# Between two transformer blocks: the last merge in PSUM, Fourier heads on unnormed tokens, both norms as one factor

## The chip, the cores and the metric

The kernel runs on one core of a Trainium2 chip. The time is the device time of one execution in microseconds (us), read as the median of several executions. TensorE (PE) multiplies matrices into PSUM, whose eight banks hold 512 f32 values per partition. VectorE (DVE) and ScalarE (ACT) read and write both PSUM and SBUF, GpSimd (POOL) works in SBUF only, and SyncE (SP) issues the transfers.

## The reference, cut to what matters

Two layers of a network, one after the other, on 256 tokens of width 1024. Around the change it computes:

```python
merged = jnp.sum(g * branch_d, axis=2)          # four branches, each times its gate
x1 = x + merged @ w_out                         # end of the first block
x2 = rms_norm(x1, final_g)                      # x1 * rsqrt(mean(x1^2) + 1e-6) * final_g
h = jnp.concatenate([meta, x2], axis=1)         # 16 meta tokens in front: 272
hn = rms_norm_2(h, norm1_g)                     # the second norm, of the normed tokens
f_in, qkv, z, ab, gate_f, gate_d = jnp.split(hn @ w_in, points, axis=-1)
fg = f_in.reshape(bsz, seq_len, 4, 128)         # four Fourier heads, then fft2 of each
```

The second block goes on with a gated delta rule over `qkv` and `ab`, and ends in a mixture of 64 experts whose weights are read from HBM.

## The kernel before, in words

Tokens stand transposed: channels in the 128 partitions, `KD` = 8 chunks of channels, tokens (`SEQ` = 256, with the meta tokens `LEN` = 272) in the free dimension. `res` holds `h`, with the 16 meta tokens in its first columns (`META`). Each engine's order is the order in which its function is written, with semaphores between them.

Every f32 product of a weight and the activations is made of three passes over rounded parts, high times low, high times high, low times high (`matmul3`, L415 to L417). So each operand is first split in a high part (a rounded copy) and a low part (the rest). Weights come in quarters of 512 KB: ACT makes the high part (L1202), POOL the low part (L2385), two quarters to a half, three halves in flight. ACT converts a half (`lead`, `lead_for`) at fixed places of its program, once the last reader of the half three before it is done. Projections go through PSUM banks 0 to 2 in turn (`PJ`), small things through banks 3 to 7 (`WK`).

The stretch of the change:

1. The last of the four branches, `br1`, is projected into four banks (two chunks each). For each, DVE multiplies by the gate (L1849), adds to `merged` (L1850), and splits the sum (L1644, L1645). The output projection `wo0` to `wo3` (48 passes each) needs all eight chunks before it can finish its first bank.
2. For each `wo` bank DVE adds the bank to `res` (L1859) and ACT squares the sum (L1325). Then PE sums the squares over the channels with a matrix of ones (`ssq2`, L455), DVE and ACT make the factor of the first norm as a full 128x256 tile (L1637, L1328, L1639), DVE applies it (L1864), ACT squares again (L1333), PE sums again (`ssq3`), DVE and ACT make the factor of the second norm (L1869, L1336, L1871), and for each chunk DVE writes the high part, the unrounded value and the low part of `hn` (L1874 to L1876).
3. PE projects the Fourier heads `fin0` to `fin3` (24 passes each, 272 columns), which wait chunk by chunk for L1876; ACT takes them out (L1339). Then comes `ab` (72 passes, three runs over 16, 128 and 128 tokens, 32 columns each) with its weight `w_ab` split by DVE (L1878), then the keys.
4. DVE takes `ab` out (L1886), ACT makes the softplus of it (L1347 to L1350), and DVE's convolutions of the keys follow (L1904, L1908).

The transfers of the second block's constants (`dft_d`, `dft_l`, `w_ab`, `tri`, `level`) wait in SP's order for the first norm (`final`, L2449).

## Time and profile before

| | |
|---|---|
| median of 3 runs | 1308.05 us (1307.49 to 1309.38) |
| the profiled execution | 1311.39 us, its span 1309.5 us |
| PE busy | 1129.7 us, 86% of the span |
| DVE, ACT, POOL busy | 489.4, 376.5, 385.2 us |
| chain that ended last | PE 60%, DMA 19%, DVE 13%, ACT 2% |
| mean granted TensorE clock | 0.925 of full speed |

The span is the profile's own time; the execution's time is 1.89 us longer. A busy share of an engine is a mean over stretches with different limits. The granted clock is told in tenths of 2.4 GHz in the page, and as a share in the view by windows (1.00 or 0.50, or a mix where it changed within the window).

### The profile page before, as it was taken

What the parts mean: (1) busy time and instruction counts of PE and PEld (TensorE: products, weight loads), DVE (VectorE), ACT (ScalarE), POOL (GpSimd) and SP (SyncE); (2) the same over time, 40 slices, a digit from 0 to 9 for tenths busy, and PEclk for the clock granted to TensorE, in tenths of its full rate; (3) what the DMA queues carried; (4) which work ended last, traced back from release to release, by engine and by line L of the source; (5) the groups of instructions that cost most, each with busy time, mean ns of one, the idle gap of its engine ahead of it and who ended that gap; (6) DMA issues with size and microseconds to landing.
All of it is one profiled execution on the core that took longest, in us unless ns stands there. A gap on an engine that the chain in (4) does not pass through costs nothing.

```text
span 1309.5 us, 20191 instructions
## 1 busy us (share of the span) xinstructions
PE 1129.7 (86%) x8332; PEld 906.7 (69%) x8332; DVE 489.4 (37%) x924; ACT 376.5 (29%) x540; POOL 385.2 (29%) x175
## 2 busy tenths in 40 slices
PE   9998999999978799988999999787767677776776
PEld 7977999999977797988888978643433333343343
DVE  3415743702262456543886332322221111221122
ACT  5524253434424175433434210301101010100101
POOL 5725668888855235433103000000000000000000
PEclk9988899999978799998999999699998888999887
DMA  7623536566644224222312137979999999999993
GB/s 260 182 65 102 156 120 198 152 180 188 181 142 129 89 82 129 73 90 65 129 65 73 59 106 312 423 280 428 428 429 428 428 427 427 428 427 429 427 429 129
DMA packets 39533, 304.30 MB, mean 232 GB/s; under 512 B 4645, under 2 KB 5029, under 8 KB 26026
## 3 DMA queue, kind: packets, MB, share of 16 engines
q1 hardware_dynamic: 39178, 302.82, 61.0%
q8 instruction: 49, 0.80, 0.3%
q10 hardware_dynamic: 288, 0.52, 0.1%
q14 instruction: 18, 0.15, 0.0%
HBM read 302.28 MB, written 1.05 MB: 232 GB/s over the span
## 4 chain that ended last, share of the span: by engine, by line
PE 60%; DMA 19%; DVE 13%; issue 2%; ACT 2%; SPq 1%; POOL 1%; DVEq 0%; ACTq 0%
PE bank L415 10%; PE bank L416 10%; PE bank L417 10%; DMA arena<-gate_up 9%; DMA weights<-gate_up 6%; PE bank L730 6%; PE bank L1150 6%; DMA arena<-down 4%; PE bank L1163 3%; DVE arena L1908 2%; PE bank L1135 1%; PE bank L1172 1%; DVE arena L2070 1%; DVE arena L2068 1%; POOL rounded L2385 1%
## 5 line engine op out<-in xcount | busy, mean ns | idle before, releaser
L2385 POOL TENSOR_TENSOR rounded<-weights,rounded 128x1024 fp32r<-128x1024 f32 x152 | 370.8, 2465 | 259.3 <-ACT rounded L1202 250.2
L415 PE MATMUL bank<-rounded 128*128 128x256 f32 (+2 forms) x784 | 227.2, 290 | 16.6 <-POOL rounded L2385 7.2
L417 PE MATMUL bank<-rounded 128*128 128x256 f32 (+2 forms) x784 | 225.5, 288 | 0.0
L416 PE MATMUL bank<-rounded 128*128 128x256 f32 (+2 forms) x784 | 225.4, 288 | 0.0
L1202 ACT ACTIVATE rounded<-weights 128x1024 fp32r<-128x1024 f32 x146 | 146.6, 1050 | 114.8 <-PE bank L417 92.6
L415 PEld LDWEIGHTS bank<-rounded 128*128 128x128 f32 (+1 forms) x784 | 151.7, 194 | 20.9 <-POOL rounded L2385 8.1
L415 PE MATMUL bank<-rounded,rounded 128*128 128x256 f32 (+3 forms) x472 | 141.3, 301 | 12.3 <-DVE rounded L1876 6.6
L416 PEld LDWEIGHTS bank<-rounded 128*128 128x128 f32 (+1 forms) x784 | 151.2, 193 | 0.3 <-issue 0.2
L417 PEld LDWEIGHTS bank<-rounded 128*128 128x128 f32 (+1 forms) x784 | 150.9, 192 | 0.3
L416 PE MATMUL bank<-rounded,rounded 128*128 128x256 f32 (+3 forms) x472 | 138.1, 294 | 0.0
L417 PE MATMUL bank<-rounded,rounded 128*128 128x256 f32 (+3 forms) x472 | 138.0, 294 | 0.0
L730 PE MATMUL bank<-arena,weights 128*128 128x256 f32 x512 | 116.0, 385 | 0.1
L730 PEld LDWEIGHTS bank<-arena,weights 128*128 128x128 f32 x512 | 97.1, 193 | 15.3 <-issue 1.5
L415 PEld LDWEIGHTS bank<-rounded,rounded 128*128 128x128 f32 (+1 forms) x472 | 94.3, 200 | 16.7 <-issue 6.5
L1135 PE MATMUL bank<-arena 128*128 128x128 f32 x512 | 73.1, 311 | 36.6 <-DVE arena L2343 36.6
L1135 PEld LDWEIGHTS bank<-arena 128*128 128x128 f32 x512 | 70.2, 224 | 42.7 <-issue 42.7
L416 PEld LDWEIGHTS bank<-rounded,rounded 128*128 128x128 f32 (+1 forms) x472 | 94.1, 200 | 0.1
L417 PEld LDWEIGHTS bank<-rounded,rounded 128*128 128x128 f32 (+1 forms) x472 | 94.0, 199 | 0.0
L1150 PE MATMUL bank<-arena 128*32 128x512 f32 x512 | 64.6, 663 | 22.1 <-DMA arena<-gate_up 20.7
L1150 PE MATMUL bank<-weights,arena 128*32 128x512 f32 x512 | 63.9, 655 | 21.8 <-DMA weights<-gate_up 19.9
L1163 PE MATMUL bank<-arena 128*32 128x512 f32 x512 | 61.4, 622 | 11.8 <-ACT arena L1597 6.6
L1172 PE MATMUL bank<-arena 128*128 128x256 f32 x256 | 59.5, 386 | 13.0 <-DVE arena L2355 13.0
(409 smaller groups left out, 1272.8 us busy)
## 6 DMA issues: line engine op xcount, KB each, us to landing
weights<-front SPq DMA_DIRECT2D x152, 512.0 KB, 4.1
weights<-gate_up SPq DMA_DIRECT2D x32, 2048.0 KB, 31.8
arena<-down SPq DMA_DIRECT2D x32, 2048.0 KB, 19.7
arena<-gate_up SPq DMA_DIRECT2D x32, 2048.0 KB, 32.1
weights<-front SPq DMA_DIRECT2D x8, 2048.0 KB, 7.8
arena<-hcatT SPq DMA_DIRECT2D x1, 1088.0 KB, 5.1
arena<-dft_l SPq DMA_DIRECT2D x1, 768.0 KB, 4.2
arena<-ln_rows SPq DMA_DIRECT2D x1, 512.0 KB
```

The source lines that it names most:

```text
L415: nc.tensor.matmul(out, a[0], b[1], start=start, stop=False)
L416: nc.tensor.matmul(out, a[0], b[0], start=False, stop=False)
L417: return nc.tensor.matmul(out, a[1], b[0], start=False, stop=stop)
L730: last = nc.tensor.matmul(f.bank[:, j * n:(j + 1) * n], w[:, c:c + P], x[:, k, :], start=k == 0, stop=k == KD - 1)
L1135: last = nc.tensor.matmul(o, m_tok[:, t, k * P:(k + 1) * P], pick_m[:, t, :], start=t == 0, stop=t == TT - 1)
L1150: last = nc.tensor.matmul(banks[3][j * CAP:(j + 1) * CAP, :], xg[:, k, j * CAP:(j + 1) * CAP], gate_up[u][j][:, k * 2 * FE:(k + 1) * 2 * F ...
L1163: last = nc.tensor.matmul(banks[5 + half][j * CAP:(j + 1) * CAP, :], hid_T[:, i, j * CAP:(j + 1) * CAP], down[j // 2][:, c:c + 512], start ...
L1172: last = nc.tensor.matmul(banks[b][:, j * SEQ:(j + 1) * SEQ], yb[:, c:c + P], pick_T, start=True, stop=True)
L1202: nc.scalar.activation(w_hi[h % SPLIT][:, quarter(q)], raw[q % RAW], ACT.Copy).then_inc(sem("w_hi"), 1)
L1908: link(nc.vector.scalar_tensor_tensor(dst[:, lo:hi], x[:, first + lo + s:first + hi + s], tap(j), dst[:, lo:hi], ALU.mult, ALU.add))
L2068: link(nc.vector.tensor_tensor(o, pairs[:, k, k + 1:32].unsqueeze(2).to_broadcast([P, below, upto]), inv[:, k, 0:upto].unsqueeze(1).to_bro ...
L2385: nc.gpsimd.tensor_tensor(lo, raw[q % RAW], hi.bitcast(f32), ALU.subtract).then_inc(sem("w_lo"), 1)
```

## The change

- **The merges.** DVE's product with the gate is written back into the PSUM bank it came from. For the last branch the sum is also left in the bank; ACT copies it out as the rounded high part, DVE subtracts for the low part.
- **The tokens between the blocks.** For each `wo` bank DVE adds `res` in place in the bank (`x1`). ACT writes it to `res`, and its rounded product with both gains (`both_g` = `final_g` times `norm1_g`) to `raw_hi_r`; DVE writes the low part `raw_lo_r`. ACT squares `x1` with and without `final_g` into banks 5 and 6, and DVE adds the pairs up in `sum_g` and `sum_x`.
- **The Fourier heads** multiply these unnormed tokens. Both norms together are one factor per token, 1/sqrt(sum_g/D + eps*(sum_x/D) + eps^2) (`factors2`), which DVE puts on each head's result as it takes it out (`take_fourier`).
- **The sums** are 128x2 columns now (`sums`), one square root and one reciprocal of 128x4; `token_rows` spreads them over the partitions (`rows12`, `rows1`). PE's order is `fin0`, `sums`, `fin1`, `rows12`, `rows1`, `fin2`, `fin3`, `ab`.
- **`hn`** is made through banks 5 and 6, high part by ACT, low part by DVE. The first norm on `res` comes last before `ab`.
- **The meta tokens** are normed at the kernel's start (`meta_n`): a square on ACT, 8 small matmuls in place of one of the products that PE runs there on zeros (`warm_up`), and 11 small DVE instructions.
- SP's transfers of the constants wait for the last `raw_lo_r` (`normed`, 16) instead of `final`.

The diff without the renumbered semaphore values; "..." also marks removed lines, which stand in the functions above:

```diff
+        SQ_BANKS, HN_BANKS = (5, 6), (5, 6)
...
+        RAW_AT = layer_base + 2 * KD * LEN
+        raw_hi_r, raw_lo_r = (rounded(RING + RAW_AT + i * KD * LEN, KD * LEN).rearrange("p (k t) -> p k t", k=KD) for i in range(2))
+        sum_x, sum_g = (arena[:, RAW_AT + 2 * KD * LEN + i * 512:RAW_AT + 2 * KD * LEN + (i + 1) * 512] for i in range(2))
+        both_g, factors2 = stat(KD), stat(2 * TT)
+        meta_n = tri[:, 0:KD * META].rearrange("p (k t) -> p k t", k=KD)
+        meta_sq = arena[:, gates_at + 1024:gates_at + 1024 + KD * META].rearrange("p (k t) -> p k t", k=KD)
...
-            warm_up(banks[5], 1)
+            f = begin("rms_rows", (2,))
+            pe.wait_ge(sem("squares"), 5)
+            for k in range(KD):
+                nc.tensor.matmul(f.bank[:, SEQ:SEQ + META], ones, meta_sq[:, k, :], start=k == 0, stop=k == KD - 1)
             pe.wait_ge(sem("rstd"), 1)
-            token_rows("rms_rows", rstd1, (2,))
+            token_rows(f, rstd1)
             warm_up(banks[5], 2)
...
+                          ready=lambda k: ("merged", 4 * 3 + 2 * (k // 2) + 2))
             hn_all = hn_hi_r, hn_lo_r
             hn_x = [m[:, :, META:] for m in hn_all]
...
+
+            def fourier_in(g):
+
+                project_T([f"fin{g}"], FIN, (raw_hi_r, raw_lo_r), LEN, per=1, column=g * P,
+                          ready=(lambda k: ("normed", KD + k + 1)) if g == 0 else None)
+
+            fourier_in(0)
+            f = begin("sums")
+            for s, src in enumerate((sum_g, sum_x)):
+                pe.wait_ge(sem("sq_pairs"), 12 + s)
+                for t in range(TT):
+                    for i in range(2):
+                        last = nc.tensor.matmul(f.bank[:, 2 * s + t:2 * s + t + 1], src[:, i * SEQ + t * P:i * SEQ + (t + 1) * P],
+                                                ones[:, 0:1], start=i == 0, stop=i == 1)
+            end(f, last)
+            fourier_in(1)
+            pe.wait_ge(sem("rstd"), 2)
+            token_rows(begin("rows12"), factors2[:, 0:TT])
+            token_rows(begin("rows1", (7,)), factors2[:, TT:])
+            fourier_in(2)
+            fourier_in(3)
             pe.wait_ge(sem("second_in"), 16 * 5)
...
+            pe.wait_ge(sem("normed"), 3 * KD + 1)
             f = begin("ab")
...
+            nc.scalar.activation(meta_sq, res[:, :, 0:META], ACT.Square).then_inc(sem("squares"), 1)
             for q in (0, 1): quarter_hi(q)
...
             norm_hi(3)
-            for q in (4, 5): quarter_hi(q)
+            quarter_hi(4)
+            act.wait_ge(sem("variance"), 2)
+            nc.scalar.activation(meta_var, meta_var, ACT.Sqrt).then_inc(sem("deviation"), 1)
...
+                lead_for(f"br{ORDER[3]}{j}")
+                act.wait_ge(sem("merged"), 4 * 3 + 2 * j + 1)
+                nc.scalar.activation(h1_hi_r[:, 2 * j:2 * j + 2, :], two(fills[f"br{ORDER[3]}{j}"].bank),
+                                     ACT.Copy).then_inc(sem("h_hi"), 1)
+            for j in range(4):
                 lead_for(f"wo{j}")
                 act.wait_ge(sem("x1"), j + 1)
...
+                x1 = two(fills[f"wo{j}"].bank)
+                if j == 0:
+                    link(nc.scalar.activation(raw_hi_r[:, :, 0:META], meta_n, ACT.Copy))
+                pair = res[:, 2 * j:2 * j + 2, META:]
+                link(nc.scalar.activation(pair, x1, ACT.Copy))
+                for i, k in enumerate((2 * j, 2 * j + 1)):
+                    last = nc.scalar.activation(raw_hi_r[:, k, META:], x1[:, i, :], ACT.Copy, scale=both_g[:, k:k + 1])
+                last.then_inc(sem("h_hi"), 1)
+                if j > 0:
+                    act.wait_ge(sem("sq_pairs"), 5 + 2 * j)
+                of_g, of_x = (two(banks[b]) for b in SQ_BANKS)
+                for i, k in enumerate((2 * j, 2 * j + 1)):
+                    last = nc.scalar.activation(of_g[:, i, :], pair[:, i, :], ACT.Square, scale=col("final_g", k))
+                last.then_inc(sem("squares"), 1)
+                nc.scalar.activation(of_x, pair, ACT.Square).then_inc(sem("squares"), 1)
+            lead_for("fin0")
+            nc.scalar.activation(spare[:, 0:1], ones[:, 0:1], ACT.Sqrt)
+            lead_for("sums")
+            f = fills["sums"]
+            act.wait_ge(sem("variance"), 5)
+            nc.scalar.activation(f.bank[:, 8:8 + 2 * TT], factors2, ACT.Sqrt).then_inc(sem("deviation"), 1)
+            for part_hi, part_raw in ((hn_hi_r, raw_hi_r), (hn_lo_r, raw_lo_r)):
+                nc.scalar.activation(part_hi[:, :, 0:META], part_raw[:, :, 0:META].bitcast(f32), ACT.Copy)
+            lead_for("fin2")
             for j in range(4):
...
+                act.wait_ge(sem("h_rows"), 4 + j + 1)
+                nc.scalar.activation(hn_hi_r[:, 2 * j:2 * j + 2, META:], two(banks[HN_BANKS[j % 2]]), ACT.Copy).then_inc(sem("h_hi"), 1)
+            lead_for("fin3")
...
                     norm_rows(j + 2)
             dve.wait_ge(sem("normed"), KD)
+            dve.sem_inc(free[sums.b], 1)
+            nc.vector.tensor_scalar(meta_var, row_bank.bank[:, SEQ:SEQ + META], 1.0 / D, EPS, ALU.mult,
+                                    ALU.add).then_inc(sem("variance"), 1)
+            link(nc.vector.tensor_tensor(both_g, cols[:, COLS["final_g"][0]:COLS["final_g"][1]],
+                                         cols[:, COLS["norm1_g"][0]:COLS["norm1_g"][1]], ALU.mult))
+            dve.wait_ge(sem("deviation"), 2)
+            meta_row = row_bank.bank[:, SEQ + META:SEQ + 2 * META]
+            link(nc.vector.reciprocal(meta_row, meta_var))
+            for k in range(KD):
+                last = nc.vector.scalar_tensor_tensor(meta_n[:, k, :], res[:, k, 0:META], col("norm1_g", k), meta_row,
+                                                      ALU.mult, ALU.mult)
+            link(last)
             dve.sem_inc(free[row_bank.b], 1)
...
+                        dve.sem_inc(free[f.b], 1)
+                        dve.sem_inc(sem("merged"), 1)
+                        continue
+                    link(nc.vector.tensor_tensor(two(f.bank), two(f.bank), g, ALU.mult))
+                    if i < 3:
+                        link(nc.vector.tensor_tensor(m, two(f.bank), m, ALU.add))
+                        dve.sem_inc(free[f.b], 1)
+                        dve.sem_inc(sem("merged"), 1)
+                        continue
+                    link(nc.vector.tensor_tensor(two(f.bank), two(f.bank), m, ALU.add))
+                    dve.sem_inc(sem("merged"), 1)
+                    dve.wait_ge(sem("h_hi"), 4 + j + 1)
+                    js = slice(2 * j, 2 * j + 2)
+                    link(nc.vector.tensor_tensor(merged_lo_r[:, js], two(f.bank), h1_hi_r[:, js].bitcast(f32), ALU.subtract))
                     dve.sem_inc(free[f.b], 1)
...
                     dve.sem_inc(sem("merged"), 1)
             for j in range(4):
                 f = got(f"wo{j}")
...
+                x1 = two(f.bank)
+                link(nc.vector.tensor_tensor(x1, x1, res[:, 2 * j:2 * j + 2, META:], ALU.add))
+                dve.sem_inc(sem("x1"), 1)
+                dve.wait_ge(sem("h_hi"), 8 + j + 1)
+                if j == 0:
+                    link(nc.vector.tensor_tensor(raw_lo_r[:, :, 0:META], meta_n, raw_hi_r[:, :, 0:META].bitcast(f32), ALU.subtract))
+                for i, k in enumerate((2 * j, 2 * j + 1)):
+                    last = nc.vector.scalar_tensor_tensor(raw_lo_r[:, k, META:], x1[:, i, :], both_g[:, k:k + 1],
+                                                          raw_hi_r[:, k, META:].bitcast(f32), ALU.mult, ALU.subtract)
+                link(last)
+                dve.sem_inc(sem("normed"), 2)
                 dve.sem_inc(free[f.b], 1)
...
+                for s, dst in enumerate((sum_g, sum_x)):
+                    dve.wait_ge(sem("squares"), 5 + 2 * j + s + 1)
+                    b = banks[SQ_BANKS[s]]
+                    if j == 0:
+                        link(nc.vector.tensor_copy(dst, b[:, :]))
+                    else:
+                        link(nc.vector.tensor_tensor(dst, b[:, :], dst, ALU.add))
+                    dve.sem_inc(sem("sq_pairs"), 1)
+
+            sums = got("sums")
+            of_g, of_x = sums.bank[:, 0:TT], sums.bank[:, TT:2 * TT]
+            nc.vector.tensor_scalar(factors2[:, TT:], of_x, 1.0 / D, EPS, ALU.mult, ALU.add)
+            link(nc.vector.tensor_scalar(factors2[:, 0:TT], of_x, EPS / D, EPS * EPS, ALU.mult, ALU.add))
+            nc.vector.scalar_tensor_tensor(factors2[:, 0:TT], of_g, 1.0 / D, factors2[:, 0:TT], ALU.mult,
+                                           ALU.add).then_inc(sem("variance"), 1)
+            dve.wait_ge(sem("deviation"), 5)
+            link(nc.vector.reciprocal(factors2, sums.bank[:, 8:8 + 2 * TT]))
+            dve.sem_inc(sem("rstd"), 1)
+            dve.sem_inc(free[sums.b], 1)
+            rows12 = got("rows12")
+
+            def hn_rows(j):
+
+                for i, k in enumerate((2 * j, 2 * j + 1)):
+                    last = nc.vector.scalar_tensor_tensor(banks[HN_BANKS[j % 2]][:, i * SEQ:(i + 1) * SEQ], res[:, k, META:],
+                                                          both_g[:, k:k + 1], rows12.bank[:, 0:SEQ], ALU.mult, ALU.mult)
+                last.then_inc(sem("h_rows"), 1)
+
+            def hn_low(j):
+
+                dve.wait_ge(sem("h_hi"), 12 + j + 1)
+                pair = slice(2 * j, 2 * j + 2)
+                link(nc.vector.tensor_tensor(hn_lo_r[:, pair, META:], two(banks[HN_BANKS[j % 2]]),
+                                             hn_hi_r[:, pair, META:].bitcast(f32), ALU.subtract))
+                dve.sem_inc(sem("normed"), 2)
+
+            def take_fourier(g):
+
+                f = got(f"fin{g}")
+                nc.vector.tensor_tensor(f_T[:, g, META:], f.bank[:, META:LEN], rms2[:, 0:SEQ], ALU.mult)
+                link(nc.vector.tensor_copy(f_T[:, g, 0:META], f.bank[:, 0:META]))
+                dve.sem_inc(free[f.b], 1)
+                dve.sem_inc(sem("f_T"), 1)
+
+            hn_rows(0)
+            hn_rows(1)
+            link(nc.vector.tensor_copy(rms2[:, 0:SEQ], rows12.bank[:, 0:SEQ]))
+            take_fourier(0)
+            hn_low(0)
+            hn_rows(2)
+            take_fourier(1)
+            hn_low(1)
+            hn_rows(3)
+            hn_low(2)
+            hn_low(3)
+            take_fourier(2)
+            take_fourier(3)
+            dve.sem_inc(free[rows12.b], 1)
+            f = got("rows1")
             for k in range(KD):
...
+                last = nc.vector.scalar_tensor_tensor(res[:, k, META:], res[:, k, META:], col("final_g", k), f.bank[:, 0:SEQ],
+                                                      ALU.mult, ALU.mult)
+            link(last)
             dve.sem_inc(free[f.b], 1)
...
+            dve.wait_ge(sem("h_hi"), 17)
+            link(nc.vector.tensor_tensor(w_ab_lo_r, w_ab, w_ab_hi_r.bitcast(f32), ALU.subtract))
             dve.sem_inc(sem("normed"), 1)
...
                 if h == 2 * FIN + 3:
-                    sp.wait_ge(sem("final"), KD)
```

How the instructions move. In DVE's order, the last of the four last merges, what follows it, and the first norm, before (bank0 to bank2 are PSUM banks, arena is SBUF, rounded a rounded part in SBUF):

```order
L1849 TENSOR_TENSOR arena<-bank1,arena 128x512
L1850 TENSOR_TENSOR arena<-arena 128x512
L1644 CAST rounded_20120_2048<-arena 128x512
L1645 TENSOR_TENSOR rounded_49952_2048<-arena,rounded_20120_2048 128x512
L1859 TENSOR_TENSOR arena<-arena,bank2 128x2x256
L1859 TENSOR_TENSOR arena<-arena,bank0 128x2x256
L1859 TENSOR_TENSOR arena<-arena,bank1 128x2x256
L1859 TENSOR_TENSOR arena<-arena,bank2 128x2x256
L1637 TENSOR_SCALAR arena<-bank7 128x256
```

And the same place in the changed kernel, from the last of the merges to the second `wo` bank:

```order
L1909 TENSOR_TENSOR bank1<-bank1,arena 128x512
L1915 TENSOR_TENSOR bank1<-bank1,arena 128x512
L1919 TENSOR_TENSOR rounded_49952_2048<-bank1,rounded_20120_2048 128x512
L1925 TENSOR_TENSOR bank2<-bank2,arena 128x512
L1929 TENSOR_TENSOR rounded_26648_2176<-arena,rounded_24472_2176 128x8x16
L1931 SCALAR_TENSOR_TENSOR rounded_26648_2176<-bank2,arena,rounded_24472_2176 128x256 x2
L1940 COPY arena<-bank5 128x512
L1940 COPY arena<-bank6 128x512
L1925 TENSOR_TENSOR bank0<-bank0,arena 128x512
```

The merge has three DVE instructions instead of four, none with two inputs in SBUF, and between two `wo` banks DVE now has five more.

On ACT, around the last `wo` bank, before:

```order
L1202 ACTIVATE rounded_4096_2048<-weights 128x1024 x2
L1325 ACTIVATE arena<-arena 128x512
L1202 ACTIVATE rounded_6144_2048<-weights 128x1024 x2
L1328 ACT_TABLE_LOAD
L1328 ACTIVATE arena<-arena 128x256
L1333 ACTIVATE arena<-arena 128x544 x4
L1336 ACTIVATE arena<-arena 128x272
```

and now:

```order
L1227 ACTIVATE rounded_4096_2048<-weights 128x1024 x2
L1363 ACTIVATE arena<-bank2 128x2x256
L1365 ACTIVATE rounded_24472_2176<-bank2,arena 128x256 x2
L1371 ACTIVATE bank5<-arena 128x256 x2
L1373 ACTIVATE bank6<-arena 128x512
L1227 ACTIVATE rounded_6144_2048<-weights 128x1024 x2
L1375 ACT_TABLE_LOAD
L1375 ACTIVATE arena<-arena 128x1
L1379 ACTIVATE bank7<-arena 128x4
```

The one square of a bank has become six instructions, all ahead of the next half of the weights, and the table of the square root is loaded by an instruction that waits for no sum.

The last DVE instructions ahead of `ab` are these in the changed kernel (before, they were the three lines L1874 to L1876 eight times, and the split of `w_ab`):

```order
L1968 TENSOR_TENSOR rounded_34840_2176<-bank5,rounded_20120_2176 128x2x256
L1968 TENSOR_TENSOR rounded_34840_2176<-bank6,rounded_20120_2176 128x2x256
L1975 TENSOR_TENSOR arena<-bank2,arena 128x256
L1976 COPY arena<-bank2 128x16
L1975 TENSOR_TENSOR arena<-bank0,arena 128x256
L1976 COPY arena<-bank0 128x16
L1996 SCALAR_TENSOR_TENSOR arena<-arena,bank7 128x256 x8
L2001 TENSOR_TENSOR rounded_37480_256<-arena,rounded_37736_256 128x256
L2009 TENSOR_TENSOR arena<-bank4,arena 16x16
```

The take-out of the heads and the first norm of `res` now stand on DVE between the last low part of `hn` and `w_ab`, for which `ab` waits.

## Rows read from the trace of the kernel before

**Rows 1.** Windows: start:end, us, PE, PEld, DVE, ACT, POOL busy (instructions), clock, DMA, GB/s
```profile
240.00:320.00 80.00, 80.00 (x669) 80.00 (x669) 24.81 (x22) 34.12 (x38) 67.22 (x28) 1.00 0.60 180
...
375.00:387.00 12.00, 4.25 (x18) 3.48 (x18) 10.91 (x11) 1.54 (x2) 5.62 (x3) 0.68 0.51 156
387.00:393.00 6.00, 5.66 (x26) 5.67 (x27) 0.23 (x1) 0.00 (x0) 0.00 (x0) 0.50 0.00 0
393.00:411.00 18.00, 18.00 (x152) 17.97 (x151) 2.21 (x4) 7.59 (x9) 12.80 (x6) 1.00 0.39 117
...
430.00:440.00 10.00, 7.79 (x25) 5.68 (x26) 9.44 (x23) 0.00 (x0) 0.00 (x0) 0.53 0.01 2
440.00:445.00 5.00, 5.00 (x26) 5.00 (x26) 0.00 (x0) 0.40 (x1) 0.00 (x0) 0.58 0.00 0
```

**Rows 2.** Timeline of DVE and POOL, last merges: start, us, engine, line, [idle before, releaser]
```profile
365.90 0.69 DVE L1849 TENSOR_TENSOR arena<-bank,arena 128x512 f32<-128x512 f32 x1 [24.09 <-PE bank L417]
...
374.24 1.83 DVE L1850 TENSOR_TENSOR arena<-arena 128x512 f32<-128x512 f32 x1
376.22 2.35 DVE L1644 CAST rounded<-arena 128x512 fp32r<-128x512 f32 x1 [0.15 <-DVE arena L1850]
378.61 2.71 DVE L1645 TENSOR_TENSOR rounded<-arena,rounded 128x512 fp32r<-128x512 f32 x1
...
386.54 0.69 DVE L1645 TENSOR_TENSOR rounded<-arena,rounded 128x512 fp32r<-128x512 f32 x1
...
375.67 5.10 POOL L2385 TENSOR_TENSOR rounded<-weights,rounded 128x1024 fp32r<-128x1024 f32 x2 [0.15 <-ACT rounded L1202]
```

**Rows 3.** Timeline, PE's first `wo` matmuls and DVE's first take-out of `wo`
```profile
376.23 0.36 PE L415 MATMUL bank<-rounded 128*128 128x256 f32 x1 [1.73 <-POOL rounded L2385]
...
381.43 0.58 PE L415 MATMUL bank<-rounded 128*128 128x256 f32 x1 [4.25 <-DVEq L1855]
...
387.34 0.58 PE L415 MATMUL bank<-rounded 128*128 128x256 f32 x1 [1.30 <-DVEq L1855]
...
393.73 0.69 DVE L1859 TENSOR_TENSOR arena<-arena,bank 128x512 f32<-128x512 f32 x1 [6.50 <-PE bank L417]
```

**Rows 4.** Timeline from the last `wo` matmul to the first of `fin0`
```profile
410.66 3.61 PE L455 MATMUL bank<-arena 128*128 128x256 f32 x16
...
412.27 1.99 ACT L1202 ACTIVATE rounded<-weights 128x1024 fp32r<-128x1024 f32 x2
...
414.28 1.28 ACT L1328 ACT_TABLE_LOAD   x1
...
416.02 1.75 DVE L1639 RECIPROCAL arena<-arena 128x256 f32<-128x256 f32 x1 [1.29 <-ACT arena L1328]
...
430.09 0.36 PE L415 MATMUL bank<-rounded,rounded 128*128 128x272 f32 x1 [4.51 <-DVE rounded L1876]
```

**Rows 5.** Windows, columns as in rows 1: `fin2` and `fin3`; `ab` at either clock
```profile
445.00:450.70 5.70, 5.70 (x48) 5.70 (x47) 0.00 (x0) 2.80 (x4) 3.83 (x2) 1.00 0.09 9
...
451.50:454.40 2.90, 2.90 (x33) 2.90 (x30) 0.00 (x0) 2.00 (x2) 1.63 (x2) 1.00 0.79 232
454.60:459.10 4.50, 4.50 (x23) 4.50 (x23) 0.00 (x0) 0.00 (x0) 2.93 (x2) 0.50 0.58 152
```

**Rows 6.** Timeline, DVE's take-out of `ab`
```profile
459.28 0.16 DVE L1886 TENSOR_TENSOR arena<-bank,arena 16x16 f32<-16x16 f32 x1 [19.56 <-PE bank L417]
```

**Rows 7.** Timeline of the kernel's start: the norm of the first block
```profile
7.93 1.95 PE L470 MATMUL bank<-arena 128*128 128x1 f32 x16
...
10.83 0.71 PE L478 MATMUL bank<-arena 128*128 128x128 f32 x4
...
11.70 1.67 DVE L1666 SCALAR_TENSOR_TENSOR bank<-arena,bank 128x256 f32<-128x256 f32 x4 [0.92 <-PE bank L478]
...
12.61 0.60 ACT L1237 ACTIVATE rounded<-bank 128x512 fp32r<-128x512 f32 x1 [2.03 <-DVE bank L1666]
```

**Rows 8.** Waits of SP's queue: who waited for whom, us in total, times, longest
```profile
SPq L2439 <- POOL rounded L2385: 538.9, 146, 33.2
```

71 lines of the change are left out of this document (16 added, 55 removed).

## The prediction

> **What bounds the kernel now.** I read the busy shares by slices first, then the waits, then the timeline from 365 to 475 us, then windows with the granted clock. From 240 to 320 us PE is busy for 80.00 of 80 us at the full clock [rows 1]: there only PE's own work counts, and the merges of the first three branches lie under it. From 375 to 387 us PE is busy 4.25 us of 12 [rows 1]. The reader is to see why: after its last `br1` matmul PE waits for the merges, and two DVE instructions of 128x512 last 2.35 and 2.71 us while POOL runs; the same split lasts 0.69 us once POOL is done [rows 2]. The output projection runs from 387.34 us on [rows 3]. Then comes a serial chain from its end (410.66 us) to the first Fourier matmul (430.09) [rows 4], then heads paced by DVE at half clock: 25 matmuls' worth of PE time in 10 us [rows 1]. SP's queue for the front weights waits for POOL, not for the memory (538.9 us in 146 waits) [rows 8], and the expert stage starts on signals of this same chain. So a microsecond cut here should be one at the end.
>
> I measure in three pieces: up to T0, the end of `wo0` (393.6 us, where DVE takes it) [rows 3]; from T0 to the first matmul of `ab` (450.8) [rows 5], 57.2 us; and `ab` itself, to 459.1 [rows 6].
>
> **Piece 1, the last merges.** Before, four DVE instructions each. Now DVE multiplies (0.69), adds (0.69), ACT copies 128x512 out of PSUM (0.60) [rows 7], DVE subtracts (0.69); with some 0.15 us for each of four hand-offs, 3.3 us a bank. From 365.9 [rows 2] the four end at 369.2, 372.5, 375.8 and 379.1. The half of the weights that ACT converts in between (2.0 us [rows 4]) fits between the second and the third copy. PE can run chunks 0 to 5 of `wo0` as they come and the last two from 379.3 instead of 387.34: 8.0 us. (The row at 376.23 names POOL as releaser of `wo0`; the bank of the second merge came free at that very moment, so I take it to be that [rows 3].)
>
> The clock: before, PE idled 1.73, then 4.25 us around six matmuls [rows 3], the clock fell to 1.2 GHz, and 26 of the 30 matmuls left to `wo0` ran at 5.66/26 = 0.22 us instead of 18.00/152 = 0.12 [rows 1]. Now one idle stretch of 2.5 us remains; I take the clock to hold. The 30 matmuls then take 3.6 instead of 6.2 us: 2.6 more. T0 is 382.9: **10.6 us** in all. That the new operation, a DVE instruction that reads and writes one bank, costs 0.69 is a choice: the nearest rows read a bank (0.69) and write another (1.67 for four halves, 0.42 each) [rows 2, 7]; the lower bound is 0.69, the upper the slowest DVE row of that size, 2.71.
>
> **Piece 2, from T0 to `ab`.** `wo0` to `wo3` stay 3 x 5.7 = 17.1 us apart (48 x 0.118) [rows 1]. ACT's work per bank grows from one square to a copy, two scaled copies and three squares, 2.8 us, and two weight quarters, 2.0: 4.8 of 5.7 us. It hides; but the half for `wo3` now starts 3 us later and is split (two POOL quarters, 5.1 us [rows 2], or less) about 1 us before PE asks. If that cover is gone, each us of delay is one on the path.
> After T0+17.1: DVE's add with its hand-off until 18.0; ACT, then done with a half, copies `x1`, then twice scaled, to 19.6; DVE's two low parts to 20.6; PE, which has done chunks 0 to 5, finishes `fin0` at 21.5. ACT's squares end at 21.0, DVE's two sums of pairs at 22.3. The eight sum matmuls are recorded as 16, 1.95 us [rows 7]; the second four start at 22.5 and end at 23.5. PE goes on with `fin1` (24 x 0.12 = 3.0 [rows 5]) to 26.5. Beside it DVE prepares the factors (24.3), ACT has loaded the root's table (1.28 [rows 4]) by then, and the factors stand at 25.1: hidden by 1.4 us. `rows12` is 0.71 [rows 7]: DVE starts at 27.3.
> Now DVE is late, and what is queued on it ahead of `ab` sets the end: products for `hn` 8 x 0.42 = 3.3 [rows 7], a copy 0.45, four low parts at 0.69 + 0.15 = 3.4, four take-outs of a head at some 0.78 (a product of 256, a copy of 16, two signals) = 3.1, 0.2 for ACT's last copy, eight products for `res` at 0.41 = 3.3, `w_ab`'s low part 0.45, hand-offs 0.35: 14.6 us, to T0+41.9. PE ends `fin3` at 33.8 and idles 8 us. 57.2 - 41.9 = **15.3 us**. What goes: the 128x256 reciprocal (1.75) and its double, two sums of 16 recorded matmuls (3.61 and more), the table load on the path (1.28) [rows 4], and the pacing of `fin0`.
>
> `w_ab`'s low part is the last instruction here with two inputs in SBUF. POOL works on the next half from about T0+36.6 to 41.3, and rows 2 show such an instruction at 2.71 instead of 0.69 beside POOL, while L1849 with an input in PSUM stayed at 0.69. I count nothing and keep 2.0 us as upper bound. The Trainium skill (SBUF — State Buffer, SBUF: two separate sides) says that a DVE instruction with two SBUF inputs and a GpSimd instruction exclude each other for a whole instruction. By that rule the sum would be up to 2 us worse where the two meet, and the saving of the merges is right as I have it.
>
> **Piece 3, `ab` itself.** Before, it began at the full clock and fell in the middle: 0.11 us per matmul of 32 columns, then 0.21 (both windows count the edges) [rows 5]. After 8 us of idle PE it now starts at 1.2 GHz, as it did after 387 us [rows 1]. Of its 48 wide-weight matmuls 26 change rate: 26 x 0.10, and 24 small ones some 0.6 in all: **3.2 us lost**. Lower bound 0, if the clock holds.
>
> **The start.** The square of the meta tokens (128x128, some 0.3 us) stands ahead of ACT's weight quarters, which had 0.2 us of slack: 0.1 lost. The root and the 10 small DVE instructions come where both wait for PE. SP's constants move ahead by as much as the chain; nobody waits for them. Merges of branches 2 and 3: nothing, PE is full.
>
> **Sum** against the profiled execution (1311.4): 10.6 + 15.3 - 3.2 - 0.1 = 22.6, so 1288.8 for a profiled execution of that kind; the runs shown have their median 3.3 below it, so 1308.05 - 22.6 = **1285.4 us**.
>
> **Rivals.**
> 1. *The short gaps drop the clock too.* PE would be near idle in `wo0` for 2.5 us and around `fin0` and the sums for 4 us with six wide matmuls between, and six matmuls did not hold it before [rows 3]. For it: that row. Against: each gap is shorter. Price: 2.6 in `wo0` and 2.0 in `fin1` (24 x 0.08); and at the start, where one of the zero products goes, up to 2. With the first two, 1290.0.
> 2. *`ab` keeps the full clock*, or PE is released earlier: 1282.2. The idle 8 us speak against it.
> 3. *Absorbed later.* A stage behind is bound by something that doesn't move with this chain. Rows 8 speak against it. If half were lost, 1296.7.
> 4. *Slower: in-place PSUM instructions are dear.* The place: the last merges (two in series per bank), DVE's x1 after the last bank, and, above 2.0 us each, the earlier merges, whose banks come every 2.9 us. At D us each the path gains 9 x (D - 0.69) + 8 x (D - 2.0); from D = 2.7 on, the gain of 22.6 is gone. At 3.5 us it would be 25.3 + 12.0 = 37.3 lost, 1322.8. Rows 2 show reads of a bank at 0.69, rows 7 writes at 0.42 per half: nothing hints at four times that.
>
> **How the numbers follow.** The forecast 0.66 (its own range 1282 to 1289), rival 1 0.20, rival 2 0.06, rival 3 0.05, rival 4 0.03. About 0.2% (2.6 us) is what a measurement of this kernel can tell from no change. Faster: all but rival 4 and a tail of rival 3, 0.95; same 0.02; slower 0.03. The range takes in rivals 1 and 2, w_ab's 2 us and hand-offs I priced by eye: 1280.5 to 1292.5.
>
> **What would show it.** In the profile of the changed kernel: the DVE instructions of the last merges at 0.69; the first matmul that follows the last merge at 379.3 us and the clock at 1.00 behind it; `wo0` ends near 383; `fin0` with one wait of about 1 to 2 us; `rows12` directly behind `fin1`; PE idle for about 8 us before `ab`, released by DVE's L2001; `ab` at about 424.8 us and 11.5 us long; and the same distances as before from `ab` to the end. The forecast is wrong if wide-matmul stretches behind `wo0` or in `fin1` show 1.2 GHz, if PE waits for weights at `wo3`, or if the distance from `ab` to the end grows.

## The result: 1292.4 us, 16.4 us faster where I forecast 22.6

| | before | changed |
|---|---|---|
| median, us | 1308.72 (1307.49 to 1309.77, 4 runs) | 1292.36 (1291.3 to 1294.23, 4 runs) |
| profiled execution: time, span, us | 1311.4, 1309.5 | 1293.09, 1291.2 |
| mean granted clock of TensorE | 0.925 | 0.929 |

The ratio is 0.987, 95% interval 0.9854 to 0.9887: 16.4 us faster, between 15 and 19. Forecast were 1285.4 (1280.5 to 1292.5): the time lies in the range, 0.1 us from its upper end and 7.0 us above the forecast itself. The profiled executions stand 18.3 us apart, 4.3 less than forecast. The other 2.6 us of the miss come from the step from a profiled execution to a median: the profiled one of before was 3.3 us above the median that I subtracted from, the changed kernel's is 0.7 above its own. Their timelines part and close again at five places; each row is the distance that a piece became shorter (+) or longer (-):

| piece | forecast, us | measured, us | from |
|---|---|---|---|
| the start, up to DVE's first merge of the last branch | -0.1 | -2.1 | 365.90, now 367.99 |
| piece 1, to DVE's take-out of `wo0` | +10.6 | +9.9 | 27.83, now 17.97 |
| piece 2, to the first matmul of `ab` | +15.3 | +14.9 | 57.17, now 42.28 |
| piece 3, `ab` | -3.2 | -2.7 | 8.38, now 11.08 |
| behind `ab`, to the end | 0 | -1.7 | 850.2, now 851.9 |
| sum | 22.6 | 18.3 | 1309.5, now 1291.2 |

### The profile after, place by place

**The last merges.** The timeline of DVE and of TensorE's first matmul of `wo` on the last bank answers to [rows 2, 3] (start, us, engine, line, [idle before, releaser]):

```profile
367.99 0.70 DVE L1909 TENSOR_TENSOR bank<-bank,arena 128x512 f32<-128x512 f32 x1 [24.50 <-PE bank L424]
...
377.51 0.70 DVE L1909 TENSOR_TENSOR bank<-bank,arena 128x512 f32<-128x512 f32 x1 [0.33 <-DVE rounded L1919]
378.25 0.70 DVE L1915 TENSOR_TENSOR bank<-bank,arena 128x512 f32<-128x512 f32 x1
379.67 0.69 DVE L1919 TENSOR_TENSOR rounded<-bank,rounded 128x512 fp32r<-128x512 f32 x1 [0.72 <-ACT rounded L1354]
385.96 0.70 DVE L1925 TENSOR_TENSOR bank<-bank,arena 128x512 f32<-128x512 f32 x1 [5.60 <-PE bank L424]
...
380.58 0.39 PE L422 MATMUL bank<-rounded 128*128 128x256 f32 x1 [1.84 <-DVEq L1921]
```

The instruction that reads and writes one bank (`bank<-bank,arena`, L1909 and L1915) takes 0.70 us. From 367.99 to 377.51 three banks pass, 3.17 us each; none of the rows of 1.8 to 2.7 us of [rows 2] is left. TensorE gets the last bank 12.59 us after the first merge; before, the same distance was 21.44 [rows 2, 3]: 8.85 us. From there to the take-out it needs 5.38 us instead of 6.39: 1.0, where I had 2.6.

**The clock.** Windows of the changed kernel (start:end, us, busy time of PE, PEld, DVE, ACT and POOL with instructions, granted clock, DMA share, GB/s), beside [rows 1, 5]:

```profile
375.00:380.00 5.00, 3.73 (x32) 3.52 (x30) 3.16 (x6) 1.74 (x4) 4.04 (x2) 1.00 0.38 120
382.00:384.00 2.00, 2.00 (x11) 2.00 (x11) 0.00 (x0) 0.00 (x0) 2.00 (x2) 0.50 0.13 53
386.00:404.00 18.00, 18.00 (x155) 18.00 (x154) 9.82 (x17) 14.54 (x26) 11.67 (x5) 1.00 0.48 143
410.00:412.00 2.00, 2.00 (x10) 2.00 (x10) 0.17 (x1) 0.39 (x2) 2.00 (x1) 0.50 1.00 330
...
429.00:439.00 10.00, 10.00 (x50) 10.00 (x48) 0.00 (x0) 0.00 (x0) 0.00 (x0) 0.50 0.15 50
```

The third figure from the end is the clock. In this stretch it is at 1.2 GHz (0.50) in three places: in the last chunks of `wo0` (TensorE had idled 1.84 us before them), in `fin1` (after `fin0`'s wait and sixteen one-column matmuls), and in all of `ab`. Only the last was in the forecast.

**From the sums to `ab`.** TensorE, then DVE, answering to [rows 4, 6]:

```profile
406.20 0.39 PE L422 MATMUL bank<-rounded,rounded 128*128 128x272 f32 x1 [1.06 <-DVEq L1934]
407.23 1.92 PE L653 MATMUL bank<-arena 128*128 128x1 f32 x16
413.62 1.05 PE L484 MATMUL bank<-arena 128*128 128x128 f32 x8
428.24 0.19 PE L422 MATMUL bank<-rounded,rounded 128*16 128x32 f32 x1 [7.55 <-issue]
```

```profile
409.99 0.18 DVE L1952 RECIPROCAL arena<-bank 128x4 f32<-128x4 f32 x1 [0.39 <-ACT bank L1379]
414.26 1.66 DVE L1960 SCALAR_TENSOR_TENSOR bank<-arena,bank 128x256 f32<-128x256 f32 x4 [4.09 <-PE bank L484]
...
424.29 3.22 DVE L1996 SCALAR_TENSOR_TENSOR arena<-arena,bank 128x256 f32<-128x256 f32 x8 [0.33 <-DVE arena L1976]
427.66 0.42 DVE L2001 TENSOR_TENSOR rounded<-arena,rounded 128x256 fp32r<-128x256 f32 x1
439.32 0.16 DVE L2009 TENSOR_TENSOR arena<-bank,arena 16x16 f32<-16x16 f32 x1 [11.24 <-PE bank L424]
```

DVE has the factors at 410.17 and then stands still for 4.09 us, because `rows12` is queued on TensorE behind all of `fin1`. From 414.26 it works without a real gap to 428.08, 13.8 us, and TensorE waits for it for 7.55 us.

**The start.** TensorE, a window with the columns of above, then DVE, answering to [rows 7]:

```profile
7.43 2.48 PE L477 MATMUL bank<-arena 128*128 128x1 f32 x16
9.78 3.57 PE L496 MATMUL bank<-arena 128*128 128x16 f32 x16
13.19 1.20 PE L484 MATMUL bank<-arena 128*128 128x128 f32 x4
```

```profile
9.80:13.10 3.30, 3.30 (x17) 3.30 (x17) 0.33 (x2) 0.77 (x2) 3.30 (x2) 0.50 0.57 181
```

```profile
10.60 0.17 DVE L1705 RECIPROCAL arena<-arena 128x2 f32<-128x2 f32 x1 [0.49 <-ACT arena L1273]
14.54 1.66 DVE L1713 SCALAR_TENSOR_TENSOR bank<-arena,bank 128x256 f32<-128x256 f32 x4 [3.77 <-PE bank L484]
```

The eight sums over the meta tokens (L496, recorded as sixteen matmuls) stand in TensorE's queue ahead of the token rows (L484). The reciprocal is ready at 10.77, but the rows start at 13.19. Before, they started at 10.83, and DVE's first product came at 11.70 instead of 14.54. The clock was down from 9.8 us on. It had fallen by the time the first of the sixteen began (9.78 us), so in this execution they ran at the low clock but did not cause its fall.

### The profile page after: what moved, and what is told of

Read it like the earlier page. It is cut to its first block, busy times and chain, and to the rows that moved or that the text cites. A ratio compares the mean times of both kernels' runs of the same rounds, so it can differ in the third digit from the quotient of the medians.

```text
span 1291.2 us, 20275 instructions
## 1 busy us (share of the span) xinstructions
PE 1120.0 (87%) x8338; PEld 903.1 (70%) x8338; DVE 480.0 (37%) x944; ACT 385.6 (30%) x566; POOL 380.5 (29%) x175
## 4 chain that ended last, share of the span: by engine, by line
PE 61%; DMA 20%; DVE 11%; issue 3%; ACT 2%; SPq 1%; POOL 1%; DVEq 0%; ACTq 0%
PE bank L422 11%; PE bank L424 10%; PE bank L423 10%; DMA arena<-gate_up 9%; DMA weights<-gate_up 6%; PE bank L755 6%; PE bank L1175 6%; DMA arena<-down 4%; PE bank L1188 3%; DVE arena L2031 2%; PE bank L1160 1%; PE bank L1197 1%; DVE arena L2193 1%; DVE arena L2191 1%; POOL rounded L2508 1%
## 5 line engine op out<-in xcount | busy, mean ns | idle before, releaser
L2508 POOL TENSOR_TENSOR rounded<-weights,rounded 128x1024 fp32r<-128x1024 f32 x152 | 366.1, 2434 | 245.5 <-ACT rounded L1227 233.6
L422 PE MATMUL bank<-rounded,rounded 128*128 128x256 f32 (+3 forms) x472 | 140.4, 299 | 14.6 <-issue 7.5
L1160 PEld LDWEIGHTS bank<-arena 128*128 128x128 f32 x512 | 68.7, 220 | 44.1 <-issue 44.1
```

Of the source, the lines that this page charges most:

```text
L422: nc.tensor.matmul(out, a[0], b[1], start=start, stop=False)
L1160: last = nc.tensor.matmul(o, m_tok[:, t, k * P:(k + 1) * P], pick_m[:, t, :], start=t == 0, stop=t == TT - 1)
L2508: nc.gpsimd.tensor_tensor(lo, raw[q % RAW], hi.bitcast(f32), ALU.subtract).then_inc(sem("w_lo"), 1)
```

## The experiments

All medians are compared with runs of the kernel before on the same chip (1309.4 to 1310.7 us there); the ratio is to those. "The changed kernel" is at 0.987. Distances inside a kernel come from one profiled execution each.

**The changed kernel again.** No edit.

> The changed kernel itself, unaltered, on this chip, so that the three others of this call stand beside it. Its first runs gave 1292.4 us, a ratio of 0.987 to the kernel before. Expected: 0.985 to 0.989 again, the start at 2 to 3 us behind, ab taken out at 439 us and 11 us after its first matmul. If one of these distances moves by over 1 us, it is noise of the execution and carries no argument.

1291.62 us, ratio 0.9867 (0.985 to 0.9885); `ab` taken out at 440.25, again 11.08 us after its first matmul.

```profile
9.66 1.94 PE L496 MATMUL bank<-arena 128*128 128x16 f32 x16
12.34 1.67 DVE L1713 SCALAR_TENSOR_TENSOR bank<-arena,bank 128x256 f32<-128x256 f32 x4 [1.61 <-PE bank L484]
...
415.18 1.66 DVE L1960 SCALAR_TENSOR_TENSOR bank<-arena,bank 128x256 f32<-128x256 f32 x4 [5.39 <-PE bank L484]
429.17 0.19 PE L422 MATMUL bank<-rounded,rounded 128*16 128x32 f32 x1 [7.56 <-issue]
```

```profile
8.60:11.90 3.30, 3.30 (x30) 3.30 (x31) 0.33 (x2) 1.72 (x3) 2.65 (x2) 1.00 0.79 317
12.10:15.30 3.20, 3.20 (x6) 1.19 (x5) 2.96 (x7) 2.03 (x3) 2.24 (x2) 0.50 0.70 180
```

Three distances don't repeat. At the start DVE's first product comes at 12.34, not 14.54, and the first merge of the last branch at 367.17, 1.3 us late instead of 2.1. The clock fell later here, at 12.0 instead of 9.8 us, when the sixteen and the rows were through: so 0.6 us (12.34 against 11.70) is what the queue alone costs DVE. And piece 2 is 44.0 us (385.14 to 429.17) where the first execution had 42.3: the clock was low for 6.8 us around `fin1` (from 408.0) where it had been low for 3.4, and DVE had its rows 30.0 us behind `wo0`'s take-out, not 28.3. Behind `ab` it is 849.7 us, not 851.9. The other executions with the same order of work have 42.5 (the gaps filled), 44.1 (the start mended) and 44.0 (TensorE kept at work). A gain within piece 2 is therefore read against the execution whose clock was low for as long.

**The meta sums alone, in the kernel before.**

```diff
-            warm_up(banks[5], 1)
...
+            for k in range(KD):
+                nc.tensor.matmul(f.bank[:, SEQ:SEQ + META], ones, meta_sq[:, k, :], start=k == 0, stop=k == KD - 1)
```

> The kernel before, with only the square of the meta tokens and their eight small matmuls at the start, in place of one product on zeros. The result of the sums is not used. Theory A (the lost time at the start is the change's own): the sixteen recorded matmuls stand in series in front of the spread factor, 0.21 us each at 1.2 GHz or 0.11 at 2.4, so this kernel is 0.8 us slower at the full clock and up to 3.0 at half; I expect +1 to +3 us, and the first projection at 16 to 17 us instead of 14.1. Theory B (the clock's chance in that one execution): no difference, within 0.5 us, and the first projection at 14.1.

1311.49 us, ratio 1.0016 (1.0 to 1.0033). Its TensorE at the start:

```profile
9.92 1.95 PE L491 MATMUL bank<-arena 128*128 128x16 f32 x16
11.71 1.20 PE L494 MATMUL bank<-arena 128*128 128x128 f32 x4
```

The sixteen records take 1.95 us at the full clock (0.12 each), where the zero product took 1.10 and nobody waited for it. The rows come at 11.71 instead of 10.83, and their 1.20 us instead of 0.71 are the lower clock. DVE starts 1.35 us late, and the copy at 28.92 is 1.47 late; at the last merges 0.36 us are left. So the edit costs 1.4 us at the start in this execution, theory A in kind, of which part is given back where I can't name the place; the interval of the ratio doesn't tell it from no change.

**The zero product taken out, nothing put in.**

```diff
             token_sums("ssq1", sq)
-            warm_up(banks[5], 1)
             pe.wait_ge(sem("rstd"), 1)
```

> The kernel before, without the one zero product of 512 columns between the token sums and the token rows at the start (recorded as two matmuls, 1.10 us together); nothing is in its place and nothing else is changed. Theory A: what the start of the changed kernel lost, it lost through the clock, because wide columns went: then the clock falls here too, between 10 and 16 us, and the first projection starts 1 to 2 us later than at 14.06, although TensorE has less to do. Theory B: it lost it through the sixteen narrow matmuls themselves, which stand on the path: then nothing is lost here, the clock holds, and the first projection starts at 14.06 or a little earlier. At the end of the kernel 1.5 us at most are to be seen: ratio 1.000 (A) to 1.001, 0.999 to 1.000 (B).

```profile
7.08 2.73 PE L470 MATMUL bank<-arena 128*128 128x1 f32 x16
10.81 0.71 PE L478 MATMUL bank<-arena 128*128 128x128 f32 x4 [1.00 <-DVE arena L1657]
```

TensorE idles for 1.00 us, the rows come at 10.81 and take 0.71, the clock stays at 1.00 up to 18 us, and the first projection starts at 14.02 (before 14.06). Theory B: the missing product costs nothing. The median (1310.97, ratio 1.0013, 0.9998 to 1.0027) tells neither way. So the start lost time through the sixteen narrow matmuls as queue ahead of the rows, and through the lower clock. Why the clock falls there is not shown. It fell between 9.8 and 12.0 us in all seven profiled executions that have the sixteen, but also in two of the four with the mended start (next run), and in none of the three without a product for the meta tokens (two with the start of before, and this one); and in the first execution of the changed kernel it was down as the sixteen began. All fourteen have sixteen one-column matmuls (the token sums) right ahead of this place.

**The start mended.** DVE adds the eight squares up in three instructions; TensorE has one product of 16 columns, and a zero product of 384 behind it.

```diff
-            for k in range(KD):
-                nc.tensor.matmul(f.bank[:, SEQ:SEQ + META], ones, meta_sq[:, k, :], start=k == 0, stop=k == KD - 1)
...
+            nc.tensor.matmul(f.bank[:, SEQ:SEQ + META], ones, meta_sq[:, 0, :], start=True, stop=True)
+            nc.tensor.matmul(banks[5][:, 0:384], warm[:, 0:P], warm[:, 0:384], start=True, stop=True)
```

> The changed kernel, with the eight meta squares added up first on DVE, one matmul instead of eight, and a product on zeros of 384 columns in its old place. Theory A: the 3.0 us that the changed kernel is behind at 30 us of the trace come back, so 1 to 3 us faster than the changed kernel (1292.4), that is 1289.5 to 1291.5. Theory B: no difference.

1288.19 us, ratio 0.9836 (0.9811 to 0.9861), by the ratios some 4 us under the changed kernel (the intervals overlap at their ends); the first merge of the last branch is at 365.87 (before 365.90), so the 2.1 us of the start are back. One execution scatters, so over all of this study: with the eight matmuls this merge came at 366.3 to 369.8 (seven executions, mean 367.9; the lowest is the kernel before with the meta sums alone), with the mended start at 364.5 to 368.2 (four, mean 365.9), with the start of before at 364.5 to 365.9 (three, one of them without the zero product, mean 365.4). The rest of the 4 us is behind `ab`, where the long part is 846.1 us here; over the fourteen profiled executions of this study it took 846 to 854, with no order by edit, and I don't count it. The clock is no clean proof of the mend either: in this execution it fell too, at 10.3 us, behind the one narrow product, and in another with this start (the three edits with the new order, below) at 9.8. That one's TensorE, and a window:

```profile
9.81 0.59 PE L503 MATMUL bank<-arena 128*128 128x16 f32 x2
9.90:13.20 3.30, 3.30 (x10) 2.34 (x10) 0.67 (x3) 0.86 (x2) 3.30 (x2) 0.50 0.57 186
```

**The merges alone, in the kernel before.** Both merges of the last branch stay in their bank and ACT copies the high part, as in the change; nothing else.

```diff
+                    link(nc.vector.tensor_tensor(two(f.bank), two(f.bank), g, ALU.mult))
...
+                    link(nc.vector.tensor_tensor(two(f.bank), two(f.bank), m, ALU.add))
```

> The kernel before, with only the merges in PSUM. Forecast of the prediction's piece 1: 10.6 us faster, of which 8.0 by the shorter merges and 2.6 by the clock. By what the changed kernel's trace shows (the last merge 8.0 us earlier, but the clock at 1.2 GHz for 3.4 us behind it) 8 to 10 us faster. Rival: if the gain of the merges needs the rest of the change (ACT's copies come behind weight conversions otherwise), under 6.

1300.99 us, ratio 0.9921 (0.9895 to 0.9946): 9 to 10 us.

```profile
378.47 0.39 PE L415 MATMUL bank<-rounded 128*128 128x256 f32 x1 [1.84 <-DVEq L1868]
```

The first merge is at 365.88, the take-out of `wo0` at 383.86: 17.98 us, as in the changed kernel (17.97). The gain of piece 1 stands alone and is carried to `ab`'s take-out (449.31 instead of 459.28, 10.0 us). The clock falls here too after the 1.84 us.

**The gaps filled.** One constant product of 512 columns before the last chunks of `wo0`, and one before those of `fin0`. The second hunk shown is for `wo0`; `fin0` has the same; `hold(n)` issues n such products.

```diff
+                            if between and i == j == 0 and k in between:
+                                between[k]()
...
-                          ready=lambda k: ("merged", 4 * 3 + 2 * (k // 2) + 2))
+                          ready=lambda k: ("merged", 4 * 3 + 2 * (k // 2) + 2), between={6: lambda: hold(1)} if half == 0 else None)
```

> The changed kernel, with one product of 512 columns on constants in each of the two short gaps of PE (before the last two chunks of wo0, and before the last two of fin0). If the short gaps let the clock fall (rival 1 of the prediction), the clock stays at 2.4 GHz behind wo0 and in fin1, and it is 2 to 4 us faster than the changed kernel: 1288.5 to 1290.5. If the clock falls for another reason (the narrow matmuls of the sums), it still falls in fin1 and only wo0 gains: 1 to 2 us. If the product itself is late, 0 to 1 us slower.

1288.75 us, ratio 0.9829 (0.98 to 0.9857). By the ratios that is 5 us under the changed kernel, more than the rows account for: they show 1.5 us in `wo0`, and the rest is not explained.

```profile
380.38 1.02 PE L430 MATMUL bank<-arena 128*128 128x512 f32 x2
382.38 0.39 PE L422 MATMUL bank<-rounded 128*128 128x256 f32 x1 [0.98 <-DVEq L1929]
```

```profile
382.00:386.00 4.00, 3.62 (x30) 3.62 (x31) 0.16 (x1) 1.33 (x2) 3.54 (x2) 1.00 0.39 128
410.00:413.00 3.00, 3.00 (x15) 3.00 (x14) 0.23 (x2) 0.83 (x5) 2.65 (x2) 0.50 0.99 357
```

In `wo0` the idle time halves, the clock stays at 1.00, and from the last bank to the take-out it takes 3.87 us (382.38 to 386.25) instead of 5.38 and, before, 6.39. That is my 2.6 us of piece 1, 2.5 by measurement. In `fin1` the fill did nothing: `fin0`'s wait was down to 0.20 us, and the clock still fell at 410.0, behind the one-column matmuls of the sums.

**TensorE kept at work before `ab`.**

```diff
+            hold(7)
             pe.wait_ge(sem("normed"), 3 * KD + 1)
```

> The changed kernel; in the 7.5 us in which TensorE waits for DVE before ab it works through 7 constant products of 512 columns (1.02 us each by the row of the same product between the chunks of wo0), which nothing reads. Theory A (my piece 3): ab is slow only because TensorE stood still before it. Then it starts at the full clock, takes 8.3 us or less instead of 11.0, and the kernel is 2.7 us faster than the changed one (some 1289.5; ratio 0.985). Theory B: in ab itself the clock falls whatever came before, because its 32-column matmuls keep TensorE as lightly busy as a gap does (before, it fell in the middle of ab). Then ab begins at 1.00 and falls after some 3 us: 8 to 9.5 us, a gain of 1.5 to 2.5 us. Theory C: the products end after DVE's last signal and hold ab up: it starts at 429 or later instead of 428.2, and the gain is under 1 us. Behind ab, the fall of the clock at 453.7 to 457.1 us, which the kernel before doesn't have, should stay in A and B: it comes from the 1.8 us wait there.

1291.96 us, ratio 0.986 (0.9837 to 0.9882): no gain to be seen in the time.

```profile
428.00:433.00 5.00, 3.51 (x41) 2.39 (x39) 2.73 (x7) 0.00 (x0) 2.56 (x2) 1.00 0.57 164
433.00:434.00 1.00, 1.00 (x10) 1.00 (x9) 0.00 (x0) 0.00 (x0) 0.00 (x0) 0.77 0.57 225
434.00:440.00 6.00, 6.00 (x30) 6.00 (x30) 0.00 (x0) 0.00 (x0) 0.00 (x0) 0.50 0.01 5
```

`ab` starts at the full clock, which falls to 0.50 about 2.6 us later, with TensorE never idle in between: 9.35 us (430.99 to 440.34) instead of 11.08. The gap is not wholly filled: the seven products end 1.49 us before `ab`, and by this run alone the later fall could still come from that. The kernel before settles it: there TensorE is busy without a gap from 444 us on, `ab` starts at 450.90 at the full clock, and the clock falls at 454.5 all the same [rows 5]. So theory B's mechanism: idle time in front isn't needed for the fall, and took the clock from the first part only. In this execution 1.7 us were lost in front (the clock low from 409.6 to 416.4, as in the second execution of the changed kernel), so the median is no proof of the 1.7 us gained in `ab`; the rows are.

**`w_ab`'s low part first.** DVE's instruction moves ahead of two take-outs and the products for `res`.

```diff
             hn_low(3)
+            dve.wait_ge(sem("h_hi"), 17)
+            link(nc.vector.tensor_tensor(w_ab_lo_r, w_ab, w_ab_hi_r.bitcast(f32), ALU.subtract))
+            dve.sem_inc(sem("normed"), 1)
             take_fourier(2)
...
-            dve.wait_ge(sem("h_hi"), 17)
-            link(nc.vector.tensor_tensor(w_ab_lo_r, w_ab, w_ab_hi_r.bitcast(f32), ALU.subtract))
-            dve.sem_inc(sem("normed"), 1)
```

> The changed kernel; DVE computes the low part of w_ab directly after the last low part of hn, ahead of the take-outs of two Fourier heads and the eight products for res, instead of behind them. No work is added or left out. Theory A: ab waits for the length of DVE's queue and for nothing else (the last stretch of the 14.6 us that I counted). Then ab starts about 4.9 us earlier, at 423.3 instead of 428.2 (eight products 3.2 us, two heads 1.3, hand-offs), and TensorE stands still for 2.6 us instead of 7.5; of this 4 to 5 us arrive at the end: 1287.5 to 1288.5, ratio 0.983. If the shorter gap also keeps the clock up, 2.7 us more: 1285. Theory B: ab is held by something else (the high part of w_ab from ACT, the bank): it starts no earlier than 426 and the gain is under 2 us. Theory C: the products for res, now behind, hold the stage behind ab: ab is early, but the distance from ab to the expert stage grows by what was won.

1287.36 us, ratio 0.9833 (0.9805 to 0.9861).

```profile
425.42 0.42 DVE L1992 TENSOR_TENSOR rounded<-arena,rounded 128x256 fp32r<-128x256 f32 x1
...
437.06 0.16 DVE L2009 TENSOR_TENSOR arena<-bank,arena 16x16 f32<-16x16 f32 x1 [6.27 <-PE bank L424]
```

```profile
426.00 0.18 PE L422 MATMUL bank<-rounded,rounded 128*16 128x32 f32 x1 [2.61 <-issue]
```

Theory A in its first half. TensorE's wait falls from 7.55 to 2.61 us, by 4.9 as worked out. `ab` starts 39.07 us after `wo0`'s take-out. In this execution `rows12` reached DVE 30.0 us behind the take-out, the clock low for 6.8 us, as in the second execution of the changed kernel; against that one (44.03) the gain is 5.0 us, and against the first (42.28, rows at 28.3) 3.2. The median is 4.3 us under that of the changed kernel beside it (1291.62), with intervals that overlap. The clock falls 0.7 us into `ab`, which takes 11.06 us: the shorter gap didn't save it.

**All three together.** Start mended, `w_ab` first, and `rows12` in the middle of `fin1` (`rows_now` waits for the factors and issues it):

```diff
-            fourier_in(1)
-            pe.wait_ge(sem("rstd"), 2)
-            token_rows(begin("rows12"), factors2[:, 0:TT])
...
+            fourier_in(1, {4: rows_now})
```

> The changed kernel with three edits: the squares of the meta tokens are added up by DVE in three instructions and TensorE has one narrow product for them instead of eight, with a zero product of 384 columns kept behind it; TensorE makes rows12 in the middle of fin1 instead of behind it; and w_ab's low part stands directly behind the last low part of hn. Nothing is left out. Theory A: the three gains lie one behind the other on the path and add up. The start gave 4.2 us alone (1288.2). rows12 early gives DVE its rows 1.5 to 2 us sooner. w_ab early gives 4 to 5 us. Together 10 to 12 us: 1280 to 1282 us, ratio 0.977 to 0.979; ab would start near 419 us with an idle TensorE of about 1 us or none before it, so that the clock holds, which gives up to 2.7 us more: 1278. Theory B: each gives its part only because another wait is behind it, and together they meet the next one (fin3 ends on TensorE at 420.7 in the changed kernel, 418.5 with the start mended, which ab can't pass): then the sum stops at 7 to 8 us, 1284 to 1285.

1285.3 us, ratio 0.9808 (0.9788 to 0.9827): theory B's size, though not by its wait. DVE and ACT:

```profile
410.25 1.67 DVE L1975 SCALAR_TENSOR_TENSOR bank<-arena,bank 128x256 f32<-128x256 f32 x4 [2.94 <-PE bank L492]
...
415.08 0.69 DVE L1983 TENSOR_TENSOR rounded<-bank,rounded 128x512 fp32r<-128x512 f32 x1 [2.30 <-ACT rounded L1396]
```

```profile
412.55 2.01 ACT L1238 ACTIVATE rounded<-weights 128x1024 fp32r<-128x1024 f32 x2 [5.03 <-PE bank L424]
414.47 1.07 ACT L1396 ACTIVATE rounded<-bank 128x512 fp32r<-128x512 f32 x2
```

DVE gets its rows sooner and stands still again, 2.30 us, for ACT's copy of `hn`. ACT had idled for 5.03 us: its queue held a half of weights in front of the copy, and that half may be written only when TensorE is through with `fin1`. TensorE's own end of `fin3` isn't the limit, it still idles 2.34 us before `ab`.

**The order of ACT's queue.** The copies of `hn` and `w_ab` go ahead of the half of weights. First in the changed kernel, with the early `rows12` alone:

```diff
-            lead_for("fin2")
             for j in range(4):
...
             nc.scalar.activation(w_ab_hi_r, w_ab, ACT.Copy).then_inc(sem("h_hi"), 1)
+            lead_for("fin3")
```

> The changed kernel with TensorE's rows12 in the middle of fin1 instead of behind it, and with ACT's copies of hn and w_ab ahead of the next half of weights. Theory A: in the changed kernel DVE stood still for 4.09 us from the reciprocal to the first product for hn, because rows12 stood behind all of fin1. Then this wait falls to about 2 us (half of fin1 and rows12 itself), ab starts 2 us earlier, and the kernel is 2 us faster than the changed one: 1289.5 to 1290.5, ratio 0.985. Theory B: the wait falls, but the queue behind it meets ACT or a bank, so that ab starts at the same distance from wo0 (42.3 us): 1291 to 1292.

1288.44 us, ratio 0.9857 (0.9836 to 0.9878). DVE's wait for `rows12` is 2.61 us instead of 4.09, there is none for ACT, and `ab` starts at 425.24, 40.97 us after `wo0`'s take-out: 1.3 us sooner than in the first execution of the changed kernel, whose clock was low in `fin1` for as long (3.4 us): theory A with two thirds of its size.

The new order in the kernel with the three edits:

> The version with all edits (1276.5 us) without the constant product between chunks 5 and 6 of wo0; so against the version with three edits (1285.3 us) it has only ACT's copies ahead of the next half of weights. Those two stood 8.8 us apart by their medians, but their profiled executions only 4.8 us at ab's take-out (432.27 and 427.48): 1.0 at wo0, 3.1 from there to the start of ab, 0.7 in ab. Theory A: the fill is worth the 1 to 1.5 us that it gives in wo0, the order 3 to 4 us up to ab, and the other 4 us are scatter of the long part behind ab, which between ab's take-out and the end took 846 to 854 us in the profiled executions of kernels that are alike there. Then this kernel lies between the two: 1278 to 1282, ratio 0.977 to 0.979. Theory B: the order of ACT's queue also mends something behind ab (the next halves, which now come in one piece of 4 us before ab ends): then it is at 1277.5 to 1278.5, and 847 to 848 us from ab's take-out to the end.

1280.95 us, ratio 0.9773 (0.9751 to 0.9794), in theory A's range, and 0.0035 or 4.6 us under the one with the old order; from `wo0`'s take-out to `ab`'s first matmul 36.03 us (386.20 to 422.23), where the old order had 38.85.

```profile
413.19 1.66 DVE L1974 SCALAR_TENSOR_TENSOR bank<-arena,bank 128x256 f32<-128x256 f32 x4 [2.52 <-PE bank L492]
422.23 0.18 PE L422 MATMUL bank<-rounded,rounded 128*16 128x32 f32 x1 [1.12 <-issue]
```

Of these 2.8 us, 2.0 are the order: from DVE's first product for `hn` to `ab` it is 9.04 us, with the old order 11.07. The other 0.8 are the clock, low for 3.4 us around `fin1` here and for 6.8 there. The part behind `ab` is 847.9 us, which theory B named; the two can't be told apart by it, since others without the edit have 846 and 847 too.

And with the constant product between the chunks of `wo0` besides:

> The previous kernel with all three edits (1285.3 us), and two more: ACT copies the high parts of hn and of w_ab before it converts the next half of weights instead of behind it, and TensorE has one constant product of 512 columns between chunks 5 and 6 of wo0. Theory A: what ate the gain of the early rows12 is ACT's queue. With all three edits, DVE waited 2.30 us for ACT's copy of hn, which stood behind a weight half that itself waited 5.03 us for the end of fin1. With the new order DVE runs through, ab starts 2.3 us sooner, at 419.0, directly behind fin3 (TensorE idle under 0.5 us before it), and one to two us more come if the clock then holds into ab. The filled gap of wo0 gives 1.5 us (16.46 against 17.97). Together 4 to 6 us below 1285.3: 1279.5 to 1281.5, ratio 0.976 to 0.978. Theory B: the half now comes 3 to 5 us later, POOL's two weight quarters end behind ab, and k0 waits for them: ab is early, but the distance from ab's take-out to the end grows by 2 us or more, and the kernel stays at 1284 to 1286.

1276.54 us, ratio 0.9762 (0.9745 to 0.9778): by its time below the range that I gave, by its ratio at the lower end of it, and the fastest version, 2.4% under the kernel before and some 14 us under the changed one. Windows, and TensorE at `ab`:

```profile
376.00:386.00 10.00, 9.01 (x73) 8.46 (x72) 3.05 (x6) 6.21 (x11) 4.76 (x3) 1.00 0.57 180
416.00:418.00 2.00, 1.09 (x29) 0.90 (x27) 1.47 (x5) 2.00 (x4) 0.97 (x1) 1.00 0.00 0
419.00:427.00 8.00, 8.00 (x39) 8.00 (x40) 3.02 (x8) 0.79 (x1) 7.36 (x4) 0.50 0.61 182
```

```profile
417.23 0.18 PE L422 MATMUL bank<-rounded,rounded 128*16 128x32 f32 x1 [0.91 <-issue]
```

From the first merge to `wo0`'s take-out 16.47 us (changed 17.97), from there to `ab` 35.81 (changed 42.28), `ab` 10.25. TensorE idles 0.91 us before `ab`. By their ratios the last two stand 0.0011 or 1.4 us apart, the size of what the constant product gives in `wo0`, but with intervals that overlap. Against the version with three edits and the old order, the profiled executions stand 8.8 us apart: 1.5 in `wo0`, 3.0 up to `ab`, 0.7 in it, 4.0 behind it (851.1 and 847.1), less 0.4 at the start. The 4.0 lie within the scatter of that part and are what my sum hadn't counted.

## Why the prediction came out as it did

**The start: wrong, and the largest miss among the pieces.** The step "The start. [...] 0.1 lost" failed. It priced ACT's square, the root and ten small DVE instructions, and left the eight matmuls of the meta sums at nothing, though they stand in TensorE's queue between the token sums and the rows that DVE waits for. Their price stood in the trace: sixteen narrow records take 1.95 us [rows 7], and TensorE had only 1.1 us there, in which nobody waited. Worked out from that row, 0.9 us and the risk of the clock. Measured are 0.6 us at DVE's first product where the clock held until the rows were through, and up to 2.8 where it fell earlier; at the last merges a mean of 2.0 against the mended start and 2.5 against that of before. The queue is shown; the cause of the clock's fall stays open, as said above.

**Piece 1: the mechanism right, one term too large.** The merges gave 8.85 (forecast 8.0: 3.17 us a bank, not 3.3). The clock in `wo0` gave 1.0, not 2.6, because it fell after the one idle stretch of 1.84 us. With that stretch filled the term measured 2.5. In-place instructions in PSUM at 0.70 end rival 4. The merges alone, in the kernel before, gave the same 9.9 us, so no other part of the change is mixed into it.

**Piece 2: right to 0.4 us in the first execution, out of two errors, and with luck.** DVE's queue is 13.8 us, not 14.6. But `rows12` reaches DVE at T0 + 28.3 instead of 27.3: `fin1` ran at 1.2 GHz, 1.3 us lost between the sums and the rows. In the second execution of the changed kernel the rows came at T0 + 30.0, and the piece gave 13.1 us, 2.2 less than forecast. That DVE, and its order, sets `ab`'s start is shown by moving one instruction: TensorE's wait fell by 4.9 us. The upper bound of 2 us for `w_ab`'s low part was not touched: it took 0.42 us. The Trainium skill (SBUF — State Buffer, SBUF: two separate sides) says that a DVE instruction with two SBUF inputs and a GpSimd instruction that reads SBUF exclude each other for a whole instruction. The run doesn't test that rule, since POOL's pair (423.09, 4.66 us) ended within 0.1 us of its start, and in no execution of the changed kernel or a version of it do the two overlap by more than 0.1 us.

**Piece 3: right in size (2.7, forecast 3.2), half right in its reason.** I put all of the loss down to the idle time in front. With TensorE kept at work, `ab` still fell to 1.2 GHz after 2.6 us and took 9.35; filling the gap down to 1.49 us gave back 1.7 us, and the clock fell in the rest of `ab` even with no gap at all, in the kernel before [rows 5]. Nine profiled executions reached `ab` at the full clock, four without any idle time before it and five after 0.9 to 2.6 us; the fall came 0.7 to 5.7 us into it, and `ab` took 6.5 to 11.1 us. Why the clock falls in these narrow matmuls, and when, is not shown.

**Behind `ab`: 1.7 us that can't be told from scatter.** I priced this part at nothing, and the second execution of the changed kernel has 849.7 us there, less than the 850.2 of before. The changed kernel's clock also fell from 453.7 to 457.1 us, in the first keys' matmuls, behind a wait of 1.77 us; DVE then waited 3.25 us for TensorE's next bank (L2062) where it waited 1.71 in the execution with the mended start, with the clock up. This is one execution each, and the fall comes and goes with no edit there, so these runs don't show the 1.7 us to be a cost of the change.

**Which case it was.** Rival 1, the short gaps drop the clock too, given 0.20: in `wo0`, in `fin1` and at the start, with prices of 2.6, 2.0 and "up to 2". With all three it would have been 1292.0 us, and the measured median is 1292.4. That they meet is partly luck: measured were 1.5 us in `wo0`, DVE's rows 1.0 us late in the first execution and 2.7 in the second, and at the start 0.6 of queue with the clock on top, and 2.6 us came from where the medians lie. The case that I gave 0.66, with its range of 1282 to 1289, missed, and by its own sign: wide matmuls behind `wo0` and in `fin1` ran at 1.2 GHz. I had left the start out of rival 1's sum, and argued against it from the gaps' length alone ("each gap is shorter"), where the row that I cited for it showed a fall after six wide matmuls between two gaps. Rivals 2 and 3 did not happen: `ab` ran at 1.2 GHz throughout, and the merges' 9.9 us at `wo0` were still 10.0 at `ab`'s take-out.

## What to carry to other kernels

A matmul that the change adds ahead of one that another engine waits for is priced like any path instruction, by its number of records and not by its columns: here sixteen narrow ones cost more than a wide product that they replaced. When a wait goes, look for what is queued in front of the waiting instruction on each engine, and on the engine behind that: DVE's wait of 4.1 us for its rows fell to 2.9, but 2.3 us came back behind ACT's weight half, and only the new order of ACT's queue freed those. Count an idle stretch on TensorE like the 1.84 us in `wo0`, and every run of narrow matmuls, as a possible fall of the clock: in `wo0` and `fin1` of the changed kernel it was low for 3.4 or 6.8 us, in which 15 to 30 matmuls ran at 0.22 instead of 0.12 us. And profile the changed kernel twice before you read a distance of 1 to 2 us: here distances moved by up to 2.2 us between two executions of the same kernel.

## What the runs showed of the hardware

- A DVE instruction of 128x512 that reads a bank and writes the same bank takes 0.70 us, as much as one that reads it and writes elsewhere (0.69).
- An f32 product of 16 columns is recorded as two matmuls of 0.12 us each at 2.4 GHz and 0.22 at 1.2 GHz, as much as a matmul of 256 columns of rounded numbers (0.12); eight products took 1.95 and 3.57 us.
- The clock fell to 1.2 GHz while TensorE was busy without a gap: at 12.0 us, after 3.3 us of narrow matmuls at a busy share of 1.00 (second execution of the changed kernel), and in `ab` with its 32 columns (kernel before, 454.5 us). With 1.00 us of idle time in place of the sixteen narrow ones it didn't fall in the one execution that has it, nor with 0.98 us behind a constant product in `wo0`; after 1.84 us in `wo0` it fell each time.
- The same code doesn't always lose the clock: with the mended start it fell in two of four profiled executions, and the point of the fall in the unmended one varied from 9.8 to 12.0 us, and DVE's first product came at 14.54 and 12.34.
